# A wider first part of w_ada, more early context units in quads, and context scans on a new timetable

## What is computed

```
mod   = silu(c) @ w_ada + b_ada            # for the latents; the same with c_ctx for the context
h     = rmsnorm(x, norm1_w) * (1 + mod[1]) + mod[0]
z     = h @ w_in                           # columns: p, q, ff, fb, i, og, gp, gh
f     = lb + (1 - lb) * sigmoid(z_f)       # ff forward, fb backward
S     = end state of the gated scan over the context, per head and direction: from k = 1 - f, log f and v = z_i
```

## Time and profile before

| | |
|---|---|
| Median of 3 runs | 2248.95 us (2247.27 to 2249.54) |
| Profiled execution, its own time | 2247.45 us |
| Its span, first to last instruction | 2245.8 us |
| Busy in the span | PE 96%, DVE 70%, ACT 43%, POOL 28% |
| DMA moved | 532.41 MB, 237 GB/s over the span |
| First latent product (end of the context part) | at 254.76 us |

### The profile page before, as it was taken

One profiled execution on the slowest core, in us unless ns is written; L12 is line 12 of the kernel. 1 busy time (PEld: TensorE's weight loads), 2 busy tenths in 40 slices (PEclk: granted clock), 3 DMA queues, 4 the chain that ended last, 5 costly groups with the idle time before them and its releaser, 6 DMA issues.

```text
span 2245.8 us, 36241 instructions
## 1 busy us (share of the span) xinstructions
PE 2161.4 (96%) x12384; PEld 1766.6 (79%) x12384; DVE 1580.9 (70%) x1999; ACT 960.5 (43%) x1152; POOL 639.5 (28%) x671
## 2 busy tenths in 40 slices
PE   4889999999999999999999999999899999999997
PEld 2679888887887887788888888788678888888884
DVE  3478555666567656766666766743689999999996
ACT  3344323233233324322222222332357777877772
POOL 0046434553554355111111111100012423324211
PEclk8999999999999999999999999999989999999999
DMA  9975563222222232677667666834499999999997
GB/s 387 401 213 155 158 201 87 86 85 86 77 86 85 85 87 95 211 229 247 218 217 251 215 219 225 273 119 148 162 368 399 410 421 419 419 421 420 419 418 259
DMA packets 324607, 532.41 MB, mean 237 GB/s; under 512 B 12448, under 2 KB 247456, under 8 KB 294720
## 3 DMA queue, kind: packets, MB, share of 16 engines
q1 hardware_dynamic: 290976, 393.91, 49.0%
q0 software_dynamic: 33568, 137.66, 17.3%
HBM read 493.74 MB, written 36.73 MB: 236 GB/s over the span
## 4 chain that ended last, share of the span: by engine, by line
PE 81%; DVE 5%; issue 2%; DMA 1%; POOL 1%; ACT 0%; DVEq 0%; ACTq 0%; POOLq 0%; SPq 0%
PE ps L714 13%; PE ps L716 12%; PE ps L715 12%; PE ps L1067 7%; PE ps L1069 7%; PE ps L1068 7%; PE ps L945 3%; PE ps L946 3%; PE ps L947 3%; PE ps L1004 2%; PE ps L1006 2%; PE ps L1005 2%; PE ps L1097 1%; PE ps L824 1%; DVE e_lo L2280 1%
## 5 line engine op out<-in xcount | busy, mean ns | idle before, releaser
L1651 DVE TENSOR_TENSOR w_lo<-raw,w_hi 128x1024 fp32r<-128x1024 f32 x272 | 348.8, 1282 | 354.7 <-ACT w_hi L1233 353.4
L1233 ACT CAST w_hi<-raw 128x1024 fp32r<-128x1024 f32 x272 | 285.1, 1048 | 582.0 <-PE ps L716 276.8
L714 PE MATMUL ps<-hl_hi,w_hi 128*128 128x512 f32 x1280 | 505.7, 395 | 3.7 <-DVE hl_lo L1717 1.4
L716 PE MATMUL ps<-hl_hi,w_lo 128*128 128x512 f32 x1280 | 498.7, 390 | 0.0
L715 PE MATMUL ps<-hl_lo,w_hi 128*128 128x512 f32 x1280 | 498.5, 389 | 0.0
L2106 DVE TENSOR_TENSOR e_lo<-e_raw,e_hi 128x1024 fp32r<-128x1024 f32 x357 | 415.9, 1225 | 15.6 <-ACT e_hi L1514 14.0
L1514 ACT CAST e_hi<-e_raw 128x1024 fp32r<-128x1024 f32 x357 | 375.7, 1054 | 105.8 <-PE ps L1069 98.5
L714 PEld LDWEIGHTS ps<-hl_hi,w_hi 128*128 128x128 f32 x1280 | 240.3, 188 | 54.7 <-issue 3.4
L716 PEld LDWEIGHTS ps<-hl_hi,w_lo 128*128 128x128 f32 x1280 | 240.2, 188 | 50.7
L715 PEld LDWEIGHTS ps<-hl_lo,w_hi 128*128 128x128 f32 x1280 | 240.5, 188 | 47.8
L1067 PE MATMUL ps<-e_hi,xe_hi 128*128 128x512 f32 x512 | 200.9, 392 | 0.1
(11 more groups left out here) (386 smaller groups left out, 3682.2 us busy)
## 6 DMA issues: line engine op xcount, KB each, us to landing
e_raw<-in_w_e SPq DMA_DIRECT2D x192, 1024.0 KB, 9.5
raw<-in_w_in SPq DMA_DIRECT2D x208, 512.0 KB, 3.8
ada<-in_w_ada POOLq DMA_DIRECT2D x64, 1024.0 KB, 6.7
ada_ring<-in_w_ada SPq DMA_DIRECT2D x32, 1024.0 KB, 15.7
raw<-in_w_out SPq DMA_DIRECT2D x32, 512.0 KB, 4.0
block_outputs<-y_sb POOLq DMA_DIRECT2D x30, 512.0 KB, 6.8
block_outputs<-osq POOLq DMA_DIRECT2D x1, 8192.0 KB, 27.1
raw<-in_w_branch_hgrn SPq DMA_DIRECT2D x16, 512.0 KB, 3.8
```

The lines of the kernel that those rows point to most:

```text
L714: mm(dst, hi, rhs_hi[:, k, :], start=(k == 0), stop=False)
L716: last = mm(dst, lo, rhs_hi[:, k, :], start=False, stop=(k == KT - 1))
L1233: act_e.copy(w_hi[:, hslot, :], raw[:, slot, :]).then_inc(hi_done, 1)
L1651: tt(w_lo[:, hslot, :], raw[:, slot, :], w_hi[:, hslot, :].bitcast(F32), ALU.subtract).then_inc(split_done, 1)
```

## The change

The columns are split at five eighths: the first part of `w_ada` has 1280 of 2048 columns of shift and scale, the second 768. The first part comes in sixteen pieces of one block k (1.25 MiB, one DMA); the second in eight pieces of two blocks (1.5 MiB). So ten of sixteen blocks of `h` can be modulated early, five pieces instead of four: fifteen early quad units instead of twelve. The order of the tiles is now `fb`, `ff`, `i`. Thirteen of the fifteen stand between the second part's eight pieces (`BEFORE`), the other two around `turn_mod(1)`. The remaining work of the first four heads is nine more quad units, 15 to 23. Heads 4 to 7 stay by head, in alternating PSUM banks. Because the quads finish four heads at once, evictions, keys, state turns and the pieces of `hl` have a new timetable in four tables. The copies of the lower bound per head on DVE and POOL are gone.

```diff
-        ADA_HALF = KT // 2
+        N_ADA = KT + 8
+        WIDE = 5 * D // 8
...
-        N_EARLY = 3 * EARLY
-        C_STATE = (18, 22, 25, 29, 32, 38, 44, U_H + 1)
+        EARLY_PIECES = 5
+        LATE_PIECES = CTX_PIECES - EARLY_PIECES
+        N_EARLY = 3 * EARLY_PIECES
+        C_REST = 3 * CTX_PIECES
+        C_ORDER = (1, 0, 2)
+        C_STATE = (25, 28, 31, 34, 38, 41, 45, U_H + 1)
+        C_EV = ((21, 18, 23), (22, 20, 25), (25, 24, 28), (28, 28, 31), (31, 32, 35), (36, 35, 38), (39, 39, 42),
+                (43, 45, 47))
+        C_KEYS = (21, 24, 27, 30, 33, 37, 40, 44)
+        HL_AT = {16: 0, 17: 1, 18: 2, 19: 3, 20: 4, 26: 5, 33: 6, 39: 7}
+        BEFORE = (0, 2, 4, 5, 7, 8, 10, 11, 13)
...
+                if q < KT:
+                    sp.dma_start(ada_ring[:, q % 4, 0:2 * WIDE].rearrange("p (m n) -> p m n", m=2),
+                                 w_ada_d[:, q, 0:2 * D].rearrange("p (m n) -> p m n", m=2)[:, :, 0:WIDE]
+                                 ).then_inc(ada_in[q % 4], 16)
+                    return
...
-            for q in range(4, ADA_HALF):
+            for q in range(4, KT):
                 load_ada(q)
-            load_ctx(0)
-            for q in range(ADA_HALF, KT):
-                n = 2 * (q - ADA_HALF) + 1
-                for s in range(n, min(n + 2, N_EARLY)):
+            for i in range(8):
+                for s in range(BEFORE[i], BEFORE[i + 1]):
                     load_ctx(s)
-                if q == KT - 1:
-                    load_ctx(N_EARLY)
-                load_ada(q)
+                load_ada(KT + i)
...
+                if q < KT:
+                    for b in range(6):
+                        m, n, wide = (b // 2, b % 2, 512) if b < 4 else (b - 4, 2, 256)
+                        c0, at = 32 * (b % 4), m * WIDE + n * 512
+                        last = mm(ps[c0:c0 + 2, OB + b // 4, 0:wide], cs[:, :, q], ada_ring[:, q % 4, at:at + wide],
+                                  start=(q == 0), stop=(q == KT - 1), tile_position=(0, c0))
...
-            for q in range(5, ADA_HALF):
+            for q in range(5, KT):
                 ada_rows(q)
             turn_mod(0)
...
-            for q in range(ADA_HALF, KT):
-                n = 2 * (q - ADA_HALF)
-                for s in range(n, min(n + 2, N_EARLY)):
+            for i in range(8):
+                for s in range(BEFORE[i], BEFORE[i + 1]):
                     quad_products(s)
-                ada_rows(q)
+                ada_rows(KT + i)
+            quad_products(BEFORE[8])
             turn_mod(1)
+            for s in range(BEFORE[8] + 1, N_EARLY):
+                quad_products(s)
...
-                own.did(dve.tensor_copy(lb_v[:], lb_all[:, h, :]))
-                own.wait()
...
-                own.did(ts(c_f[:, 0, :], c_sig[:, 0, :], lb_v[:, 1:2], lb_v[:, 0:1], ALU.mult, ALU.add))
+                own.did(ts(c_f[:, 0, :], c_sig[:, 0, :], lb_all[:, h, 1:2], lb_all[:, h, 0:1], ALU.mult, ALU.add))
```

More of the change, by code:

```diff
@@ L536, in load_ctx @@
                 sp.wait_ge(split_done, s + 1)
-                if s < N_EARLY:
+                if s < C_REST:
                     i, kq = quad_unit(s)
@@ L565, in _ @@
             sp.dma_start(masks_in[:], level_masks).then_inc(consts_in, 16)
-            for s in range(N_EARLY + 1, U_H):
+            for s in range(BEFORE[8], U_H):
                 load_ctx(s)
@@ L689, in ada_rows @@
             def ada_rows(q):
[L691 to L698, removed]
+                pe.wait_ge(ada_in[q % 4], 16 * (q // 4 + 1) if q < KT else 64 + 32 * ((q - KT) // 4 + 1))
+                if q < KT:
[4 more added lines that the diff above has]
+                                  start=(q == 0), stop=(q == KT - 1), tile_position=(0, c0))
+                else:
+                    for kk in range(2):
+                        k = 2 * (q - KT) + kk
+                        for b in range(4):
+                            c0, at = 32 * b, (4 * kk + b) * 384
+                            last = mm(ps[c0:c0 + 2, OB, 0:384], cs[:, :, k], ada_ring[:, q % 4, at:at + 384],
+                                      start=(k == 0), stop=(k == KT - 1), tile_position=(0, c0))
                 last.then_inc(ada_mm, 1)
@@ L737, in ctx_products @@
                 dst = ctx_bank(h, i)
-                if s >= N_EARLY and h:
-                    pe.wait_ge((c_sig_f, c_sig_b, c_v_ev)[i], h)
+                if half == 0:
+                    pe.wait_ge((c_sig_f, c_sig_b, c_v_ev)[i], (2, 4, 5, 6)[h - EARLY])
                 pe.wait_ge(split_done, split_value(s))
@@ L1253, in _, with hl_hi_piece @@
             w_hi_unit(0)
-            for n in range(CTX_PIECES // 2):
+            for n in range(EARLY_PIECES):
                 ctx_hi(n)
-            for s in range(1, N_EARLY + 1):
+                if n == 1:
+                    w_hi_unit(1)
+            for s in range(2, N_EARLY):
                 w_hi_unit(s)
             mod_out(1)
-            for n in range(CTX_PIECES // 2, CTX_PIECES):
+            w_hi_unit(N_EARLY)
+            for n in range(EARLY_PIECES, CTX_PIECES):
                 ctx_hi(n)
+            def hl_hi_piece(n):
+                act_e.wait_ge(h_rdy, n + (EARLY_PIECES + 1 if n < EARLY_PIECES else CTX_PIECES + 1))
+                act_e.copy(hl_hi[:, 2 * n:2 * n + 2, :], xT_lat[:, 2 * n:2 * n + 2, :]).then_inc(h_hi, 1)
             def ctx_copies(hd):
@@ L1291, in _ @@
                         act_e.copy(c_vT[:, h % 2, :], ctx_bank(h, 2)).then_inc(c_v_ev, 1)
-                if h >= EARLY and (i, half) in ((0, 0), (2, 0)):
-                    hl_hi_piece(2 * (h - EARLY) + i // 2)
+                if s in HL_AT:
+                    hl_hi_piece(HL_AT[s])
             def mix(hd, idx):
@@ L1694, in _ @@
             dve.wait_ge(xT_dve, 2 * (NTOK + NCTX))
-            for n in range(4):
+            for n in range(EARLY_PIECES):
                 modulate(xT_ctx, n, 1)
```

160 lines of the change are left out of this document (86 added, 74 removed).

## The result

| | Before | After |
|---|---|---|
| Median (4 runs each) | 2248.11 us (2247.27 to 2249.54) | 2261.47 us (2260.1 to 2264.15) |
| Ratio, 95% interval | 1 | 1.0057 (1.0045 to 1.0069) |
| Profiled execution | 2247.45 us | 2260.21 us |
| Its span | 2245.8 us | 2258.6 us |
| End of the last early w_ada pass, T1 | 63.34 | 83.10 (81.64 + 1.46) |

The change is slower, as forecast, but by 12.8 us between the profiled executions instead of 6.5. The time lies outside the range. The busy times of the whole say little: the page's line is close to that of the earlier trace rows, PE 5 us higher.

A forecast was written before the change was run, and what follows sets the result against it. PE is busy 96% of the span, but the w_ada and x stream bounds 24 to 60 us. Terms 18.1 + 1.0 - 1.5 - 7.7 - 3.4 give +6.5 us, median 2255.5; range of all 2246 to 2260.5.

The forecast's parts named there:

- Bytes ahead of T1, pass shorter by 0.4: Up to the last early w_ada pass: 4.19 MB more cost 10.2 us, less a shorter last pass; +9.8.
- Holes: DMA queue runs empty twice before the last early w_ada pass ends, for 5.0 and 3.3 us; +8.3.
- T1 to the first product: Last early w_ada pass to first context product: more small copies, turns and sums; +1.0, bounds 0.5 and 1.5.
- First product to T2: First context product to the last w_ada pass of all: thirteen units, eight shorter passes, 52.2 us for 53.65; -1.5.
- T2 to the end of unit 17: Last w_ada pass of all to unit 17's end: 18.1 us for 25.80, with a 2.9 us wait for w_lo; -7.7.
- The rest of the context: From unit 18 on: 6.2 us of PE idle, waits for POOL's keys and hl_lo go, 2.8 of new waits; -3.4.
- Behind it: Behind the context scans: nothing edited and PE full, so the rest moves rigidly; 0.
- The path up to the scans: Start to context products: bytes and two queue holes end the last early w_ada pass 18.1 us later, first product +1.0 more.
- The text's signs: Profile signs: DMA under 250 GB/s at 24-28 and near 54 us, first product at 88-91, first 512-column product 6-8 later.
- the second hole: Near 54 us: w_ada piece 9's request waits for pass 5, behind the turning of x tiles 3 to 5; 3.3 us.
- The rival of the full queue: Early requests for x tiles keep the DMA queue from running dry, both holes go: -8.3, 2247.2 us; chance 0.16.
- The rival of half clock: PE at half clock at the last early pass (+1.4), its turn (+0.5) and the middle (+2.3): 2259.7 us; chance 0.14.

The follow-up runs named there:

- e6_near: Changed kernel with six slots of 1.25 MiB in place of four, and w_ada passes of PE put between the x tiles: 2250.57 us, ratio 1.0011.
- e3_small: Kernel before the change, with only w_ada's first half read in pieces of one block (1 MiB) in place of two: 2261.50 us, ratio 1.0054.
- e4_ring: Changed kernel with its 1.25 MiB pieces in a ring of six slots in place of four: 2254.86 us, ratio 1.0026.
- e5_near4: Changed kernel, still four slots, with two w_ada passes of PE after x tile 3 and two after x tile 4: 2256.79 us, ratio 1.0047.
- e8_hl: Changed kernel with latent pieces 5, 6, 7 cast at units 25, 34, 37 in place of 26, 33, 39: 2260.52 us, ratio 1.0049.
- e1_state: Changed kernel with the context turn of head 5 one unit later (42, not 41): 2258.46 us, ratio 1.0050.
- e9_combo_hl: e7_combo with the latent pieces moved as in e8_hl: 2246.66 us, ratio 0.9995 to the kernel before.
- e2_mid: Changed kernel with weight unit 16's halves put ahead of the last context casts on ACT and DVE: 2260.74 us, ratio 1.0054.
- e7_combo: Changed kernel with the edits of e6_near, e1_state and e2_mid together: 2247.80 us, ratio 0.9999 to the kernel before.

## Why the prediction was right and wrong

| Step | Forecast | Measured |
|---|---|---|
| Bytes ahead of T1, pass shorter by 0.4 | +9.8 | +9.4 (T1 at 72.74 in `e6_near`) |
| Holes | +8.3 | +10.4 (83.10 against 72.74) |
| T1 to the first product | +1.0 | +0.6 (6.90 against 6.29) |
| First product to T2 | -1.5 | -1.1 (52.56) |
| T2 to the end of unit 17 | -7.7 | -8.0 (17.8) |
| The rest of the context | -3.4 | +0.8 (106.5) |
| Behind it | 0 | +0.6 |

**The path up to the scans was right.** Both holes opened at the places and for the reasons that the text gave: SP's request for x tile 3 at 27.4, tied to the turning of tile 0, and pass 5 behind the turning of tiles 3 to 5. `e3_small` shows that holes cost as much as the queue loses, `e4_ring` and `e5_near4` close one each, and `e6_near` both. The text's signs held, but for the last early pass, which ended 0.1 us past its 80 to 83, and the first latent product, 12.2 us later and not 6 to 8.

**The step that failed is "The rest": -3.4 was +0.8.** POOL's waits did go, as told. But the forecast left PE 2.8 us of idle in this stage, and it has 6.4 (106.5 - 100.13), and its busy time is 0.65 us longer (99.48 before); the unit at half clock alone is 1.1. The step priced DVE's levels 4 to 8 of the first heads against the slack of a unit, and left out head 5. That head's keys, three groups of levels and turn stand in five units in a row (37 to 41), with a latent piece among them, while every other head has a free unit between its last levels and its turn. So the 3.0 us wait is on the turn itself. Half of it is DVE's work on the latent piece, and as much is DVE standing still behind ACT's sigmoids of the next head (1.54 us in `e8_hl`). The 4.2 us are the 3.0 of this wait, 0.6 by which the other waits (3.4 us, for `w_lo` and for keys) exceed the 2.8 that the step priced, and the 0.65 of busy time. Which of those other waits stand where the step had put its own was not followed. `e1_state` and `e8_hl` take back 2.45 and 2.9 us of it; `e9_combo_hl`, with the order at the middle too, 5.4.

**The holes were under-sized by 2.1 us.** Of it, 0.7 is the second hole (4.0 us by the changed kernel's rows from 52 to 58, not 3.3). The first was nearly right: from 22 to 30 us the rows have 1.13 MB, 2.7 us of full queue, so 5.3 us were lost against 5.0. About 0.6 is the rate from 30 to 40 us, 386 GB/s where I took 411, and 0.4 that from 58 to 64. I had taken the full rate from the moment at which the queue starts again. But SP asks for x tiles 3, 4 and 5 one by one, each when another tile has been turned. In the changed kernel they go out at 27.41, 30.12 and 32.82 us, 2.7 us apart, and one is 2.5 us of full queue, so the queue holds hardly more than one transfer there. That this is the loss is an argument; no run separates it.

**Slips in the sum.** Thirteen units at the text's own 5.94 us a pair are 38.6 us, not 38.3, so the term of the first product to T2 is -1.2, close to the -1.1 measured. From moved to seen the text's own times give 2.0 us (44.1 to 46.08), not 2.1. Neither matters to the result. The fit that the text cites from the Trainium skill, "DMA: Bandwidth & Descriptors", Anatomy of one DMA, is one for DMAs that GpSimd issues, and these are SP's; the sum does not use it.

**The rival of the full queue** is `e6_near`. It wins 10.4 us at the first product and 10.0 in span.

**The rival of half clock** came true as a fact and not as a cost in the places that it named. PE did stand at half clock while it waited for pieces:

```profile
64.00:68.00 4.00, 2.73 (x12) 0.38 (x12) 0.00 (x0) 0.00 (x0) 0.00 (x0) 0.50 1.01 406
```

A pass took 2.73 us there instead of 1.46. That is still less than the 3.2 us in which a piece arrives, and before T1 the clock was back (1.46 at 81.64). Of the last seven passes two ran cold, behind waits of 2.0 and 1.1 us, and the last five at full clock, behind waits of 1.5 to 1.7. The Trainium skill, "TensorE: Matmul & The Clock Gate", HAM oscillation, tells of a loop whose products start cold each time, since its wait for data is longer than they are and also long enough to bring the clock down; the trace here has such a fall for the two passes and not for the five. In the middle the clock stayed at 1.00 from 142.6 to 160.4 us through the wait of 2.34. What the half clock cost beyond the forecast was behind the wait for head 5, 1.1 us, at a place that the rival had not named.

**The sum.** 12.8 us are 9.4 + 10.4 + 0.6 - 1.1 - 8.0 + 0.8 + 0.6, which is 12.7. The 6.2 us between that and the forecast are 4.2 of the rest, 2.1 of the holes and 0.6 behind the context, less 0.7 of the other terms. The range's upper end, 2260.5, had no room for the holes and the rest to be too low together. That 0.6 behind the context is within the scatter of that part.

## What to carry to other kernels

When pieces get smaller, the bytes ahead in the ring shrink with them: multiply slots by piece size, compare it with the time that the consumer is held up by something else, and while the stream is the bound, expect every missing byte back as delay. More slots and a consumer that is not blocked behind other work are two separate remedies, and here both were needed. In a timetable written by hand, follow the head with the least slack through to its turn, not the first one, and price work between two of its steps as part of it, with the waits of the engine that feeds it. And look at the pace of PE in every profile before comparing two: a clock that differs between executions moves times that look like the edit's.

## What the runs showed of the hardware

- What the queue lost came back as delay within 0.8 us in ten profiles. Among the kernels with five eighths, in the table's order and against `e6_near`, the first product was later by 10.4, 9.9, 11.5, 5.1, 5.4, 1.7, 10.4, 0.4 and 4.4 us, where the queue was short by 9.9, 9.4, 11.0, 5.1, 5.2, 1.3, 9.6, -0.2 and 3.7. The tenth is `e3_small` against before.
- Behind the first hole the queue ran at 384 to 387 GB/s from 30 to 40 us in all four profiles that have the hole and turn x tile 1 at full pace (after, `e1_state`, `e5_near4`, `e8_hl`), against 416 and 420 in `e6_near` and `e9_combo_hl`. SP's requests come one by one there, and no run tells that from a slow restart.
- PE's pace while it turned x tile 1 differed between profiles with the same instructions: 1.94 us in seven of them, 3.62 to 3.65 in `e2_mid`, `e3_small`, `e4_ring` and `e7_combo`. `e2_mid` and the changed kernel are the same program up to there, so it is a matter of the execution and not of the edits. SP's request for x tile 4 waits for that turning, and the DMA rate followed: 238 to 334 GB/s from 32 to 36 us in the four, 383 to 427 in the seven. The stretches of `e7_combo`, then of `e9_combo_hl`:

```profile
28.00:30.00 2.00, 1.75 (x9) 1.78 (x10) 0.80 (x2) 0.59 (x2) 0.00 (x0) 0.50 1.01 415
32.00:36.00 4.00, 3.34 (x34) 2.22 (x36) 2.51 (x4) 2.37 (x5) 0.00 (x0) 0.97 0.90 326
```

```profile
28.00:30.00 2.00, 1.94 (x16) 1.71 (x16) 0.58 (x2) 0.36 (x2) 0.00 (x0) 1.00 1.01 413
32.00:36.00 4.00, 4.00 (x38) 1.38 (x38) 1.29 (x2) 3.00 (x4) 0.00 (x0) 1.00 1.02 420
```

At 0.50, the 1.2 GHz level, PE turns 9 blocks in the time of 16, and the queue falls to 326 GB/s a little later. What set the clock there was not tried.

- The clock column can miss this. In `e3_small` it reads 1.00 from 24 to 40 us, while x tiles 1 and 2 took 3.65 us each. There the pace of the instructions is the surer sign.
